# Fetching the down weights of experts 4 and 5 without waiting for the first gather, in a two-layer transformer kernel

## The chip, the cores and the metric

One core of a Trainium2 chip runs the kernel. The metric is the device time of one execution in microseconds (us). Runs of one kernel agree within about 0.3%.

## What is computed

The input x is (1, 512, 1024) float32: 512 tokens. Two layers follow each other. Each is a mixer (attention of two kinds side by side) and then a mixture of experts, both with a plain residual:

```python
for layer in range(2):
    h = h + mixer(rmsnorm(h, attn_norm[layer]))      # even_mixer, then odd_mixer
    h = h + hierarchical_moe(rmsnorm(h, ffn_norm[layer]), ...)
return rmsnorm(h, final_norm)
```

The experts are 32 per layer, in 4 groups of 8. Each token goes to the best group and there to its best 2 experts, with weights:

```python
g_idx = argmax(t @ w_group + b_group)
top_v, top_i = top_k(router logits of that group, 2)
gates = p_group * softmax(top_v)          # zero for all other experts
a, u = t @ w_gate[e], t @ w_up[e]         # 1024 -> 256
y = y + (silu(a) * u * gates[e]) @ w_down[e]   # 256 -> 1024
```

Each expert's three matrices are 1 MB each, so that a layer's experts are 96 MB of weights that are read once.

## The kernel before, in words

It is written by hand in five instruction streams, one per engine, which meet at semaphores: SyncE (sp) issues the large transfers, GpSimd (pool) the gathers, scatters and small loads, TensorE (pe) multiplies, VectorE (dve) and ScalarE (act) do the rest. Instructions of an engine go out in program order, so a wait holds up all that stands behind it in its own stream.

**Attention and routing.** After a layer's attention, `mixer_out` on TensorE multiplies by the output weights (line 825), and between these products transposes the new rows (line 846), makes the router logits (line 860) and counts the ranks of the tokens in their experts (lines 872, 873, 880). Matmuls whose result nobody reads (`stay_busy`, line 889) fill the waits. VectorE turns the logits into indices (its last step is line 1479). The normed, transposed rows that the router multiplies lie in the buffer hnT.

**Experts.** Expert e has 64 places for rows. For each expert in turn:

- GpSimd gathers its rows from DRAM (line 587) into one of four buffers Xg. The first four gathers are issued together once the indices are there; each further one when its buffer is free.
- TensorE transposes them (line 940); VectorE copies them out with the gain (line 1564); TensorE multiplies by the gate and up weights (lines 951, 952), ScalarE and VectorE make the hidden rows, TensorE transposes these (line 958) and multiplies by the down weights (lines 964, 966); VectorE copies the result (line 1579) and GpSimd scatters it to DRAM (line 592).
- TensorE starts an expert when its gate and up weights have landed. Rows of expert e+1 are transposed while expert e is under way.

**Weights and their slots.** There are six slots for experts' weights (`SLOT_W`, `SLOT_D`). Each is a 2 MB buffer for gate and up and a 1 MB one for down. The down slots of experts 4 and 5 are the two halves of hnT, which is why they can only be loaded once the router logits of the layer are done (semaphore s_lg). `load_gate_up` (line 413) issues two transfers of 1 MB, `load_down` (line 418) one. Expert e, from 6 on, is loaded into the slot of an earlier expert: its gate and up weights when TensorE has done that expert's gate and up products (s_gu), its down weights when the down products are done (s_y).

**The place of the change.** `before_routing` holds SyncE's stream between attention and experts. It ends with the gate and up weights of expert 5, a wait for the first gather of the layer (semaphore s_g[0], counted up by 16 when a transfer has landed), a wait for the layer's four chunks of router logits, and the down weights of experts 4 and 5. Behind it stands `experts`, whose first entry waits for TensorE to be done with expert 0's gate and up weights. The function runs once per layer, so the wait stands twice in the program.

Of the kernel before, what the change touches and what calls it, by code (L numbers as in the profile page):

```python
# [93 lines left out]
def trunk(nc, x, attn_norm, ffn_norm, final_norm, e_w_in, e_b_f, e_w_out, o_w_in, o_q_norm, o_kv_norm,  # L94
# [71 lines left out]
    with ctx:  # L166
# [3 lines left out]
        def sem(name):  # L170
            return ctx.enter_context(nc.semaphore(name))
# [181 lines left out]
        s_g = [sem(f"rows_gathered{i}") for i in range(4)]  # L353
# [35 lines left out]
        def _(sp):  # L389
# [5 lines left out]
            def load_cols(buf, dst, src, c0, width):  # L395
                sp.dma_start(dst, src[:, :, c0:c0 + width]).then_inc(s_ld[buf], 48)
# [13 lines left out]
            def load_gate_up(lay, e):  # L410
                gate_up, _, done, _ = expert_slot(lay, e)
                for v, at, count in ((wg_v[lay], 0, 16), (wu_v[lay], 2048, 32)):
                    sp.dma_start(gate_up[:, at:at + 2048].rearrange("p (h x) -> p h x", h=2), v[e])\  # L413
                      .then_inc(done[0], count)

            def load_down(lay, e):
                _, down, _, done = expert_slot(lay, e)
                sp.dma_start(down, wd_v[lay][e]).then_inc(done[0], 16)  # L418

            def before_routing(lay, w_out):  # L420

                sp.wait_ge(s_qk, 64 * (lay + 1))
                load_cols("Q", flatQ.rearrange("p (k n) -> p k n", k=KD), w_out, 0, 512)
                load_cols("K", flatK.rearrange("p (k n) -> p k n", k=KD), w_out, 512, 512)
                sp.wait_ge(s_pv, 8 * (lay + 1))
                load_down(lay, 3)
                sp.wait_ge(s_og, 8 * lay + 4)
                load_gate_up(lay, 4)
                rows = h_dram[lay].rearrange("(s h) d -> s (h d)", h=2)
                for c in range(C):  # L430
                    sp.wait_ge(s_oga, 8 * lay + 5 + c)
                    sp.dma_start(rows[128 * c:128 * c + 128, :], h[:, c, :]).then_inc(s_hst, 16)
                sp.wait_ge(s_og, 8 * lay + 8)
                load_gate_up(lay, 5)
                sp.wait_ge(s_g[0], 16 * (8 * lay + 1))
                sp.wait_ge(s_lg, C * (lay + 1))
                load_down(lay, 4)
                load_down(lay, 5)
# [64 lines left out]
            sp.wait_ge(s_pj, 24)  # L503
            load_gate_up(0, 3)
            before_routing(0, ewout_v)
            experts(0)
            sp.wait_ge(s_gu, 24)
# [22 lines left out]
            sp.wait_ge(s_pj, 52)  # L530
            load_gate_up(1, 3)
            before_routing(1, owout_v)
            experts(1)
            further_tiles(1)
# [1205 lines left out]
```

## Time and profile before

| | |
|---|---|
| median of 3 runs | 1150.05 us (1149.61 to 1153.0) |
| the profiled execution | 1149.53 us |
| its span, first to last instruction | 1147.7 us |
| PE busy | 1029.5 us, 90% |
| VectorE, ScalarE, GpSimd busy | 402.8, 255.2, 161.0 us |
| moved by DMA | 268.65 MB, mean 234 GB/s |
| granted TensorE clock, mean | 0.965 of full |

The span runs through attention of layer 0, its experts (from about 346 us to 582 us), attention of layer 1, its experts (from about 882 us to 1118 us) and the final norm. PE's share is an average: a TensorE that is busy 90% of the time may still be waiting at the places that set the end. For the stages the profile gives windows (busy time of each engine, the granted clock, the DMA engines' share and GB/s within a stretch), and the chain of waits that ended last, which tells at each moment what the end hung on.

### The profile page before, as it was taken

The page shows a single profiled execution, that of the slowest core. Times are in us where ns is not written, and L with a number is a line of the kernel's source. Part 1 is how long each engine was busy: PE and PEld are TensorE (multiplying, and loading weights), DVE is VectorE, ACT ScalarE, POOL GpSimd, SP SyncE. Part 2 cuts the span into 40 slices and gives each one's busy share as a digit, 9 for nine tenths or more (in the row PEclk, how much of TensorE's full clock was granted, in tenths as well). Part 3 has the DMA queues.
Part 4 walks back from the last instruction along what each step waited for, and adds up shares of the span by engine and source line. Part 5 has one row for each costly group of instructions (what it writes and reads, how often), then busy time and mean ns, then how long its engine had stood idle before and what let it go on. Part 6 is the DMA issues. An engine that isn't in the chain of part 4 may idle for free.

```text
span 1147.7 us, 13123 instructions
## 1 busy us (share of the span) xinstructions
PE 1029.5 (90%) x5160; PEld 549.3 (48%) x5160; DVE 402.8 (35%) x1115; ACT 255.2 (22%) x667; POOL 161.0 (14%) x170
## 2 busy tenths in 40 slices
PE   5999999999999999988838998989999999998890
PEld 3344644464455555444414647446455555554440
DVE  3122810362264322222234326458035432322225
ACT  3121710262121111000012226447012111110012
POOL 2000000001003333222111000000102233222210
PEclk9999999999999999999978999999999999998995
DMA  9610202215238999999978210023325999999975
GB/s 330 228 60 25 75 1 110 74 74 190 92 128 339 411 408 410 410 410 411 413 298 289 74 73 1 9 100 116 122 110 194 382 410 410 411 411 410 411 303 230
DMA packets 78814, 268.65 MB, mean 234 GB/s; under 512 B 13664, under 2 KB 17872, under 8 KB 69786
## 3 DMA queue, kind: packets, MB, share of 16 engines
q1 hardware_dynamic: 67056, 248.17, 55.3%
q0 software_dynamic: 11696, 19.62, 4.9%
q8 instruction: 42, 0.69, 0.2%
q14 instruction: 20, 0.16, 0.0%
HBM read 261.41 MB, written 23.10 MB: 248 GB/s over the span
## 4 chain that ended last, share of the span: by engine, by line
PE 71%; DMA 17%; DVE 5%; SPq 4%; ACT 2%; issue 1%; DVEq 0%; POOLq 0%; ACTq 0%
PE bank L735 13%; PE bank L951 12%; DMA W<-in_moe_w_up 10%; PE bank L825 10%; PE bank L747 9%; PE bank L964 7%; PE bank L766 5%; PE bank L777 2%; PE bank L940 2%; PE bank L793 2%; SPq L418 2%; DMA Q<-in_moe_w_up 2%; DMA oT<-in_moe_w_up 2%; PE bank L1071 2%; SPq L413 1%; PE bank L958 1%
## 5 line engine op out<-in xcount | busy, mean ns | idle before, releaser
L951 PE MATMUL bank<-W,K 128*64 128x256 f32 x768 | 186.1, 398 | 27.5 <-DMA W<-in_moe_w_up 25.7
L952 PE MATMUL bank<-W,K 128*64 128x256 f32 x768 | 186.2, 398 | 0.0
L951 PEld LDWEIGHTS bank<-W,K 128*64 128x64 f32 x768 | 105.6, 142 | 87.8 <-DMA W<-in_moe_w_up 29.5
L735 PE MATMUL bank<-hnT,W 128*128 128x512 f32 x336 | 145.1, 593 | 0.8 <-ACT hnT L1145 0.8
L1559 DVE SCALAR_TENSOR_TENSOR PT<-bank,V,PT 64x256 f32<-64x256 f32 x64 | 31.4, 490 | 273.8 <-ACT PT L1209 273.8
L952 PEld LDWEIGHTS bank<-W,K 128*64 128x64 f32 x768 | 105.6, 142 | 0.0
L735 PEld LDWEIGHTS bank<-hnT,W 128*128 128x128 f32 x336 | 63.5, 190 | 80.5 <-issue 79.5
L964 PE MATMUL bank<-D,PT 128*64 128x512 f32 x192 | 92.6, 604 | 0.7 <-ACT PT L1213 0.7
L966 PE MATMUL bank<-D,PT 128*64 128x512 f32 x192 | 92.6, 604 | 0.0
L587 POOL DMA_INDIRECT K<-rows,V x64 | 66.4, 1037 | 147.7 <-DVE V L1479 124.1
L1209 ACT ACTIVATE PT<-bank,V 64x256 f32<-64x256 f32 x64 | 29.9, 468 | 254.4 <-PE bank L952 251.8
L766 PE MATMUL bank<-K,Q 128*128 128x256 f32 (+3 forms) x256 | 70.4, 417 | 6.1 <-ACT K L1158 3.4
L1173 ACT ACTIVATE P<-P,nm 128x256 f32<-128x256 f32 (+3 forms) x128 | 68.3, 535 | 14.6 <-DVE nm L1353 14.1
L747 PE MATMUL bank<-W,hnT 128*128 128x512 f32 (+2 forms) x256 | 71.4, 440 | 0.0
L825 PE MATMUL bank<-K,oT 128*128 128x512 f32 x128 | 59.2, 600 | 0.0
L825 PE MATMUL bank<-Q,oT 128*128 128x512 f32 x128 | 56.5, 594 | 1.4 <-ACT oT L1189 1.4
L592 POOL DMA_INDIRECT expert_rows<-V x32 | 32.6, 1018 | 163.9 <-DVE V L1579 163.9
L592 POOL DMA_INDIRECT expert_rows<-K,V x32 | 32.5, 1017 | 163.7 <-DVE K L1579 163.7
L747 PEld LDWEIGHTS bank<-W,hnT 128*128 128x128 f32 x256 | 40.4, 190 | 31.1 <-issue 31.1
L1213 ACT ACTIVATE PT<-bank 128x128 f32<-128x128 f32 x64 | 17.8, 278 | 156.0 <-PE bank L958 156.0
L1353 DVE CUSTOM_DVE_ANT_0 P<-bank,cst 128x128 f32<-128x128 f32 (+1 forms) x96 | 46.0, 489 | 15.0 <-PE bank L766 13.8
L766 PEld LDWEIGHTS bank<-K,Q 128*128 128x128 f32 x256 | 40.7, 190 | 21.6 <-DVE nm L1353 6.0
(226 smaller groups left out, 1431.2 us busy)
## 6 DMA issues: line engine op xcount, KB each, us to landing
D<-in_moe_w_down SPq DMA_DIRECT2D x48, 1024.0 KB, 22.1
W<-in_moe_w_gate SPq DMA_DIRECT2D x48, 1024.0 KB
W<-in_moe_w_up SPq DMA_DIRECT2D x48, 1024.0 KB
hnT<-in_moe_w_down SPq DMA_DIRECT2D x16, 1024.0 KB, 21.7
W<-in_e_w_in SPq DMA_DIRECT2D x5, 2048.0 KB
Q<-in_moe_w_gate SPq DMA_DIRECT2D x8, 1024.0 KB
Q<-in_moe_w_up SPq DMA_DIRECT2D x8, 1024.0 KB
oT<-in_moe_w_gate SPq DMA_DIRECT2D x8, 1024.0 KB
```

What stands on the lines that cost most here:

```text
L587: pool.indirect_dma_start(out=dst, out_offset=None, in_=h_dram[lay], in_offset=bass.IndirectOffsetOnAxis(ap=idx_col, axis=0), bounds_check ...
L592: pool.indirect_dma_start(out=y_dram[lay], out_offset=bass.IndirectOffsetOnAxis(ap=idx_col, axis=0), in_=src, in_offset=None, bounds_check ...
L735: last = nc.tensor.matmul(b[:, :], w[:, k, 128 * fb:128 * fb + 128], hnT[:, k, :], start=(k == 0), stop=(k == KD - 1))
L747: last = nc.tensor.matmul(b[:, at:at + width], hnT[:, k, 128 * c:128 * c + 128], w[:, k, c0:c0 + width], start=(k == 0), stop=(k == KD - 1))
L766: nc.tensor.matmul(bank[b % 3][:, 0:n], Q[:, u, 128 * i:128 * i + 128], K[:, kv, k0:k0 + n], start=True, stop=True).then_inc(s_qk, 1)
L825: last = nc.tensor.matmul(bank[g % 2][:, :], oT[:, k, 128 * c:128 * c + 128], w_out[half][:, k, :], start=(k == 0), stop=(k == KD - 1))
L951: nc.tensor.matmul(bank[2 + e2][0:64, 0:256], xt, w[:, at:at + 256], start=first, stop=end)
L952: last = nc.tensor.matmul(bank[2 + e2][64:128, 0:256], xt, w[:, 2048 + at:2304 + at], start=first, stop=end)
L964: nc.tensor.matmul(bank[5 + e2][0:64, :], hT[e2][:, 64 * c:64 * c + 64], d[:, 1024 * c:1024 * c + 512], start=(c == 0), stop=(c == 1))
L966: last = nc.tensor.matmul(bank[5 + e2][64:128, :], hT[e2][:, 64 * c:64 * c + 64], d[:, 1024 * c + 512:1024 * c + 1024], start=(c == 0), st ...
L1173: nc.scalar.activation(blk, blk, ACT.Exp, bias=nm[:, b % 8:b % 8 + 1], scale=-1.0, accum_out=den[:, b % 8:b % 8 + 1]).then_inc(s_exp, 1)
L1353: nc.vector.tensor_tensor_reduce(out=P[:, u % 2, p_col(f, i):p_col(f, i) + n], in0=bank[b % 3][:, 0:n], in1=cst[:, at + width - n:at + wid ...
```

## The change

The wait for the first gather is taken out; the wait for the router logits stays. Both layers use the function, so two waits go.

```diff
                 sp.wait_ge(s_og, 8 * lay + 8)
                 load_gate_up(lay, 5)
-                sp.wait_ge(s_g[0], 16 * (8 * lay + 1))
                 sp.wait_ge(s_lg, C * (lay + 1))
                 load_down(lay, 4)
                 load_down(lay, 5)
```

On no engine does an instruction move. On SyncE, at the end of `before_routing` in layer 0, where oT is the gate and up slot of expert 5, hnT the down slots of experts 4 and 5, and the last W row the gate weights of expert 6, the rows read (a minus is before, a plus the change):

```order
 L413 DMA oT<-in_moe_w_gate 128x2x1024 [waits mixer_projected]
 L413 DMA oT<-in_moe_w_up 128x2x1024
-L418 DMA hnT<-in_moe_w_down 128x2048 [waits router_logits,rows_gathered0]
+L418 DMA hnT<-in_moe_w_down 128x2048 [waits router_logits]
 L418 DMA hnT<-in_moe_w_down 128x2048
 L413 DMA W<-in_moe_w_gate 128x2x1024 [waits gate_up_done]
```

Of the two semaphores before the first down load only that of the router logits is left; layer 1 reads the same.

## Rows read from the trace of the kernel before

**Rows 1.** The page: GB/s moved in 40 equal slices of the span.

```profile
GB/s 330 228 60 25 75 1 110 74 74 190 92 128 339 411 408 410 410 410 411 413 298 289 74 73 1 9 100 116 122 110 194 382 410 410 411 411 410 411 303 230
```

**Rows 2.** Windows, the long stretches: busy us (instructions) per engine, clock, DMA share, GB/s.

```profile
361.00:578.00 217.00, 200.17 (x1358) 107.39 (x1356) 61.79 (x116) 21.89 (x59) 59.61 (x60) 0.98 1.02 409
...
897.00:1104.00 207.00, 193.65 (x1298) 103.53 (x1294) 59.82 (x112) 21.14 (x57) 56.68 (x56) 0.97 1.02 410
```

**Rows 3.** Windows of 1 us, same columns (PE, PEld, DVE, ACT, POOL first).

```profile
343.00:344.00 1.00, 1.00 (x3) 0.48 (x3) 0.62 (x5) 0.31 (x2) 0.39 (x1) 1.00 0.45 172
344.00:345.00 1.00, 1.00 (x3) 0.38 (x2) 0.83 (x7) 0.00 (x0) 0.71 (x1) 1.00 0.07 29
345.00:346.00 1.00, 1.00 (x4) 0.38 (x2) 0.97 (x5) 0.00 (x0) 0.98 (x1) 1.00 0.49 135
...
349.00:350.00 1.00, 1.00 (x13) 0.79 (x11) 0.44 (x1) 0.00 (x0) 1.00 (x1) 1.00 0.99 418
...
360.00:361.00 1.00, 1.00 (x6) 0.65 (x8) 0.48 (x1) 0.47 (x1) 0.00 (x0) 1.00 0.07 25
...
362.00:363.00 1.00, 1.00 (x8) 0.44 (x6) 0.44 (x1) 0.02 (x1) 0.00 (x0) 1.00 1.01 414
...
880.00:881.00 1.00, 1.00 (x3) 0.38 (x2) 0.83 (x7) 0.00 (x0) 0.74 (x1) 1.00 0.21 70
```

**Rows 4.** Timeline of SyncE's DMA queue: start us, us, line, transfer.

```profile
346.73 0.81 SPq L418 DMA_DIRECT2D hnT<-in_moe_w_down  x2
352.09 0.38 SPq L413 DMA_DIRECT2D W<-in_moe_w_gate  x1
...
360.01 0.37 SPq L413 DMA_DIRECT2D W<-in_moe_w_gate  x1
...
882.60 0.82 SPq L418 DMA_DIRECT2D hnT<-in_moe_w_down  x2
```

**Rows 5.** The chain that ended last: start us, us, what.

```profile
337.01 1.22 PE bank L860 x8
...
343.61 3.10 DMA K<-rows,V
346.76 0.76 PE bank L940 x4
...
879.63 2.95 DMA K<-rows,V
```

**Rows 6.** Waits of SyncE, whole span: us in total, times, longest.

```profile
SPq L418 <- DMA K<-rows,V: 16.7, 2, 8.4
```

**Rows 7.** The page's DMA issues: count, size of each, median us to landing.

```profile
hnT<-in_moe_w_down SPq DMA_DIRECT2D x16, 1024.0 KB, 21.7
```

**Rows 8.** Line 587, layer 0's fourth and fifth gather: issue and time to landing.

```profile
L587 POOL DMA_INDIRECT K<-rows,V x1: 998/998/998, 347.6 to 347.6; - x1
DMA to landing us min/median/max: 7.4/7.4/7.4
...
L587 POOL DMA_INDIRECT K<-rows,V x1: 1357/1357/1357, 349.0 to 349.0; - x1
DMA to landing us min/median/max: 6.4/6.4/6.4
```

**Rows 9.** Timeline of PE: start us, us, line, [idle before, releaser].

```profile
342.82 3.68 PE L889 MATMUL bank<-cst 128*128 128x512 f32 x8
...
1019.85 0.43 PE L951 MATMUL bank<-W,K 128*64 128x256 f32 x1 [2.02 <-DMA W<-in_moe_w_up]
...
1020.60 0.63 PE L951 MATMUL bank<-W,K 128*64 128x256 f32 x1
...
1023.96 0.38 PE L951 MATMUL bank<-W,K 128*64 128x256 f32 x1
...
1024.18 0.38 PE L951 MATMUL bank<-W,K 128*64 128x256 f32 x1
...
1079.25 0.43 PE L951 MATMUL bank<-W,K 128*64 128x256 f32 x1 [1.86 <-DMA W<-in_moe_w_up]
```

## The prediction

> **What bounds the kernel now.** I read the forty slices of the page first. In each layer the DMA engines move 408 to 413 GB/s through one long stretch, slices 14 to 20 and 33 to 38 [rows 1], and nowhere else as much. Those are the expert stages. The stage windows say the same of them: DMA share 1.02 at 409 and 410 GB/s over 217 and 207 us [rows 2], while PE is busy for 200 of the 217 us. Once such a stretch has begun, its end is fixed by its bytes. What counts is therefore when the stretch **begins**, and who decides that.
>
> The windows of 1 us at the head of the first layer's stage answer it [rows 3]. The transfers for expert 5 run out in window 343:344 (172 GB/s), 344:345 is nearly empty (29 GB/s), 349:350 is full again (418 GB/s) with the down weights of experts 4 and 5 and then the gate and up weights of expert 6. At 360:361 the engines are empty a second time (25 GB/s), and from 362:363 (414 GB/s) they stay full to the end. So the long stretch starts with the loads of expert 7. SyncE issues those at 360.01 [rows 4], when PE has finished the gate and up product of expert 1. All slots are full before that: a weight load can't come earlier than PE frees a slot.
>
> When does PE start? The chain of waits reads [rows 5]: the last router product at 337.01, routing on VectorE, the gather of expert 0's rows issued at 343.61, on the chain for 3.10 us as DMA, and PE's transposes of those rows at 346.76. In the second layer the same gather is issued at 879.63 and holds the chain for 2.95 us. From there everything up to expert 7's loads is PE's own chain. The first gather is on the path that sets the end, in both layers.
>
> **The change part by part.** It removes one wait of SyncE per layer. The waits of the DMA queue's own engine price it as seen from SyncE: 16.7 us, twice, at most 8.4 [rows 6]. No instruction is added or moved on any engine. SyncE's next wait there is for the router logits, whose last four of eight products stand in the 1.22 us from 337.01 [rows 5], so the two loads go out at about 338.3 in place of 346.73, and at about 874.4 in place of 882.60 [rows 4].
>
> *Gain on the weights: nothing.* Each load is 1024 KB [rows 7], the two together 2.10 MB, 5.1 us at 410 GB/s. Now they fill the hole behind expert 5's transfers, from about 343.5 to 348.7. But the next weight load (expert 6, 352.09) waits for PE's first product and the one after it (expert 7, 360.01) for the second [rows 4]. The engines were empty before expert 7's loads even with the down weights sent late (25 GB/s in 360:361), so sending these early only makes the second hole longer. The down weights themselves are late for nobody: they are used by experts 4 and 5, five experts after the one now starting, and no wait of PE for them shows at either place. Cover for this zero: PE's chain from gather 0 to the end of expert 1's product, some 13 us from 346.76 to 360. If the cover were gone, the 5.1 us would be a gain, see the rivals.
>
> *Cost on the gather.* Gather 0 is issued at 343.61 into engines that were about to fall empty. Afterwards it is issued just as the down weights begin to move, and they keep the engines full for 5 us. The trace of before has gathers issued beside such a load [rows 8]: the fourth of the same layer, issued at 347.6, took 7.4 us to land, the fifth, issued at 349.0, took 6.4. Against 3.10 us that is 3.3 to 4.3 us more. This is the upper bound, because those two had a load beside them for all of their way. For gather 0 the load ends at about 348.7, or 349.5 with the bytes of the gathers; then it finds empty engines again. Issued at 343.61 and landed soon after 349.5, it is 2.9 us later than 346.7. In the second layer expert 5's transfers run until about 880, past the issue of the gather (880:881 is the first slack window, 70 GB/s [rows 3]), so that the down weights with the gathers last to about 886: landing 3.5 us later than the present end, 879.63 + 2.95 = 882.6. The lower bound is zero, if the gather's few bytes pass between the weights; a gain below zero is excluded, as the same gather can't be faster with more beside it. I take 2.9 and 3.5, nearest to the rows of loaded gathers and cut by the length of the load: 6.4 us.
>
> Here the Trainium skill speaks against a cost (DMA: Bandwidth & Descriptors, section Queues, rings and completion order): each DMA engine takes turns between the queues that have work, a packet at a time. By that rule a short gather on a queue of its own would be held up by about its own size in others' packets, some tenths of a microsecond, and the sum would be close to zero. The rows of the 7.4 us and 6.4 us gathers don't agree with so small a delay, though they don't show where the time is spent. I go by the rows.
>
> *Cost on PE's clock.* PE fills its wait for the gather with products that nobody reads, 3.68 us from 342.82 [rows 9], so up to 346.5. Now it sits idle for about 3 us more behind them, then does 0.75 us of transposes and waits again for VectorE. What a gap can do shows in the second layer, in the same rows: after 2.02 us of waiting the product runs at full speed, then from 1020.60 to 1023.96 eight pairs of matmuls take 3.36 us, where the next pair starts 0.22 us after the one before (eight of them 1.76): 1.6 us lost at the lower granted clock, 1.2 GHz. A gap of 1.86 us at 1079.25 has no such slow products behind it, so a gap of that size may cost or not. The bounds are 0 and 1.6 us per layer. A 3 us gap is longer than both, but part of the slow time may lie inside the gap where it costs nothing; I take half, 0.8 us per layer, 1.6 us in all. It adds in full, as the first product is on PE's chain.
>
> *Sum.* 2.9 + 3.5 + 1.6 = 8.0 us. The profiled execution took 1149.53 us (span 1147.7 plus 1.8 around it); it stands 0.5 us under the median of the runs, 1150.05. From the execution 1157.5, from the median 1158. I forecast **1157.5 us**, 0.65% slower. Nothing later gives it back: the stretch after 362 has its full bytes to move at 410 GB/s whenever it starts, and it starts later by what PE starts later.
>
> **The rivals.**
> *The gather gets its turns (not slower).* Gather 0's packets pass between those of the weights and it lands within 1.5 us of now. For it: its bytes are few (135 GB/s in 345:346 [rows 3], when gathers alone moved, are 135 KB in that microsecond), and the load ends soon. Against it: the 6.4 and 7.4 us of rows 8. The price is 0 to 1.5 us per layer, no clock loss: 1150 to 1153, around 1151. It decides below 1.7 us per layer, where two layers stay within what can be told from no change. Chance 0.18.
> *The hole is filled and pays (faster).* If the engines were the only limit of the stage, moving 2.10 MB into an empty place would take up to 5.1 us from each layer: 1149.5 − 10.2 = 1139.3, or part of it. The point from which it decides: expert 7's loads would have to stand in the queue before it runs empty. They are issued at 360.01 and the windows show the queue at 25 GB/s there, so it speaks against itself by 1 to 2 us in each layer. Chance 0.05.
> *Both costs in full (slower still).* The gather takes the whole 7.4 us, because weights that were begun are finished first, and PE's first product runs wholly at the lower clock: 2 × (4.3 + 1.6) = 11.8, so 1161.3. For it: the rows of the gathers as they stand. Against it: the load beside gather 0 ends after 5 us. Chance 0.15.
> *The change does nothing* would need SyncE to be held at that place by something else. The other wait is over at 338.3, so I count this under the first rival.
>
> **How the numbers follow.** My own case, a gather 2.3 to 4.0 us late per layer with some or no clock loss, is 1154 to 1160.5 and has 0.62. A measurement of this kernel can tell about 0.3%, 3.5 us, from no change; that is the band of "same", 1146.6 to 1153.5. Slower: 0.62 + 0.15 = 0.77; same: 0.18; faster: 0.05. The range goes from 1151, in the middle of the first rival, to 1161.5, which takes in the full price of the third; outside are the faster case and the lower half of the first rival, some 0.15 together.
>
> **What would show it.** In the changed profile the two down loads are issued near 338.3 and 874.4, and the wait for the gather is gone from SyncE. The engines are full to about 349, then empty until expert 6's loads. The chain shows the first gather as DMA for 5.5 to 7 us in each layer, PE's first transposes near 349.7 and 886.1, expert 7's loads near 363.5 and 899, and the long stretch beginning 3 to 4 us later with unchanged length. A row of slow first products would show the clock term. I am wrong if gather 0 still lands in about 3 us, or if the long stretch begins no later, or ends sooner than it began later.

## The result and the profile after

The changed kernel took 1163.46 us in the median (1162.2 to 1164.68), the kernel before beside it 1150.64 us. The ratio is 1.0105, with a 95% interval of 1.0093 to 1.0118: about 12 us slower. The forecast was 1157.5 us with a range up to 1161.5. The direction was right, the loss was larger than the range allowed for. The profiled execution has a span of 1161.8 us, 14.1 more than before. That is more than the 12 us of the ratio because the profiled execution of before (1149.53 us) is among its fastest: 27 executions of that kernel beside the first experiments took 1149.4 to 1156.7 us, a wider spread than the 0.3% given at the start. Differences of marks below are therefore those of single executions, and the ratios say what a change costs on the average. In the rows of the changed kernel the line numbers behind the removed line are lower by one: its line 586 is 587 of before, 939 is 940, 950 is 951.

The timeline of SyncE's DMA queue in both layers, start and duration in us, answers to [rows 4]:

```profile
338.42 0.82 SPq L418 DMA_DIRECT2D hnT<-in_moe_w_down  x2
357.73 0.38 SPq L413 DMA_DIRECT2D W<-in_moe_w_gate  x1
367.33 0.37 SPq L413 DMA_DIRECT2D W<-in_moe_w_gate  x1
...
881.77 0.86 SPq L418 DMA_DIRECT2D hnT<-in_moe_w_down  x2
900.49 0.38 SPq L413 DMA_DIRECT2D W<-in_moe_w_gate  x1
910.09 0.37 SPq L413 DMA_DIRECT2D W<-in_moe_w_gate  x1
```

The down weights go out 8.3 us earlier, as the change says. The loads of expert 7 go out at 367.33 instead of 360.01, 7.3 us later. The chain of waits (start, us, what) answers to [rows 5]:

```profile
343.83 7.06 DMA K<-rows,V
350.94 0.76 PE bank L939 x4
351.73 0.70 DVE K L1563
352.57 0.66 PE bank L950
353.26 0.39 PE bank L950
...
362.65 0.41 PE bank L950
363.08 0.41 PE bank L950
...
887.10 6.59 DMA K<-rows,V
893.74 0.76 PE bank L939 x4
```

The gather of expert 0's rows now holds the chain for 7.06 us in the first layer and 6.59 in the second, where it held it for 3.10 and 2.95. The pieces at line 950 are the matmuls of TensorE's gate and up products, as far as each holds the chain: 0.39 to 0.41 us, where at full clock it is 0.20 to 0.21. That happens in the product of expert 0 (from 352.57) and again in that of expert 1 (from 362.65), in both layers. The windows of 1 us (busy time of PE, PEld, DVE, ACT, POOL, then the granted clock, DMA share, GB/s) show the load and the clock, against [rows 3]:

```profile
349.00:350.00 1.00, 0.00 (x0) 0.00 (x0) 0.00 (x0) 0.00 (x0) 0.00 (x0) 1.00 0.99 371
350.00:351.00 1.00, 0.06 (x1) 0.06 (x1) 0.00 (x0) 0.00 (x0) 0.00 (x0) 1.00 0.45 162
...
353.00:354.00 1.00, 1.00 (x8) 0.66 (x6) 0.62 (x2) 0.00 (x0) 0.00 (x0) 0.50 0.33 78
...
363.00:364.00 1.00, 1.00 (x8) 0.59 (x6) 0.00 (x0) 0.00 (x0) 0.00 (x0) 0.50 1.01 414
...
366.00:367.00 1.00, 1.00 (x12) 0.57 (x8) 0.00 (x0) 0.00 (x0) 0.00 (x0) 1.00 0.00 0
...
370.00:371.00 1.00, 1.00 (x10) 0.66 (x11) 1.00 (x7) 0.28 (x1) 0.14 (x1) 1.00 0.98 406
```

TensorE has nothing at all in 349:350, the clock column stands at 0.50 (1.2 GHz) in 353:354 and in 363:364, and the DMA engines are empty in 366:367, before expert 7's loads. The long stretch begins at about 369.5 instead of 361.9. It runs at the same rate as in [rows 2], so its length is unchanged:

```profile
369.00:586.00 217.00, 200.10 (x1359) 107.45 (x1356) 61.16 (x115) 21.87 (x59) 59.59 (x60) 0.98 1.02 409
```

So the span divides at four marks per kernel. Before: first gather issued 343.61, landed 3.10 later, expert 7's loads 13.30 after that (360.01); in the second layer 879.63, 2.95, 13.29 (895.87). After: 343.83, 7.06, 16.44 (367.33); 887.10, 6.59, 16.40 (910.09). What lies between is the same: from 360.01 to 879.63 is 519.62, from 367.33 to 887.10 is 519.77; from expert 7's loads of the second layer to the end 251.83 and 251.71. The 14.1 us are therefore 3.96 + 3.64 = 7.6 for the gathers, 3.14 + 3.11 = 6.25 between landing and expert 7's loads, where nothing but the slow products has changed, and 0.25 in all elsewhere. The 6.25 are of two parts: from expert 6's loads to expert 7's it is 9.60 us in both layers instead of 7.92, which is 1.68 each for the second product; the first product is left with 1.46 and 1.43.

### The profile page after: what moved, and what is told of

It reads as the page before. It is cut to its first block, busy times and chain, and to the rows that moved or that the text cites. A ratio compares the mean times of both kernels' runs of the same rounds, so it can differ in the third digit from the quotient of the medians.

```text
span 1161.8 us, 13121 instructions
## 1 busy us (share of the span) xinstructions
PE 1036.0 (89%) x5160; PEld 551.8 (47%) x5160; DVE 402.8 (35%) x1115; ACT 255.1 (22%) x667; POOL 160.4 (14%) x170
## 4 chain that ended last, share of the span: by engine, by line
PE 70%; DMA 18%; DVE 4%; SPq 4%; ACT 2%; issue 1%; DVEq 0%; ACTq 0%
PE bank L950 13%; PE bank L734 12%; DMA W<-in_moe_w_up 10%; PE bank L824 10%; PE bank L746 9%; PE bank L963 6%; PE bank L765 5%; PE bank L939 2%; PE bank L776 2%; SPq L418 2%; DMA Q<-in_moe_w_up 2%; PE bank L792 2%; DMA oT<-in_moe_w_up 2%; PE bank L1070 2%; SPq L413 1%; PE bank L957 1%
## 5 line engine op out<-in xcount | busy, mean ns | idle before, releaser
L950 PE MATMUL bank<-W,K 128*64 128x256 f32 x768 | 192.4, 408 | 27.6 <-DMA W<-in_moe_w_up 25.8
L951 PE MATMUL bank<-W,K 128*64 128x256 f32 x768 | 192.4, 408 | 0.0
L950 PEld LDWEIGHTS bank<-W,K 128*64 128x64 f32 x768 | 108.5, 146 | 91.5 <-DMA W<-in_moe_w_up 29.4
L951 PEld LDWEIGHTS bank<-W,K 128*64 128x64 f32 x768 | 108.5, 146 | 0.0
L1172 ACT ACTIVATE P<-P,nm 128x256 f32<-128x256 f32 (+3 forms) x128 | 68.3, 535 | 14.6 <-DVE nm L1352 14.1
L939 PE MATMUL bank<-cst,K 128*128 128x128 f32 x256 | 47.9, 309 | 8.0 <-DMA K<-rows,V 8.0
L1563 DVE TENSOR_TENSOR K<-bank,V 128x512 f32<-128x512 f32 x64 | 44.3, 692 | 21.8 <-PE bank L939 20.0
```

The lines of the kernel that those rows point to most:

```text
L939: last = nc.tensor.transpose(bank[e2][:, 128 * k:128 * k + 128], src.rearrange("p (x k) -> p k x", k=4)[:, k, :], ident)
L950: nc.tensor.matmul(bank[2 + e2][0:64, 0:256], xt, w[:, at:at + 256], start=first, stop=end)
L951: last = nc.tensor.matmul(bank[2 + e2][64:128, 0:256], xt, w[:, 2048 + at:2304 + at], start=first, stop=end)
L1172: nc.scalar.activation(blk, blk, ACT.Exp, bias=nm[:, b % 8:b % 8 + 1], scale=-1.0, accum_out=den[:, b % 8:b % 8 + 1]).then_inc(s_exp, 1)
```

## The experiments

The theory to test: the weights gain nothing by being early; the first gather is late because of the load beside it; the slow products come from the gap in which TensorE waits for it. The rivals: the gather alone costs, or the slow clock alone, or the begin of the long stretch isn't what sets the end. All ratios are to the kernel before on the same chip, whose median beside these runs was near 1152 us. A ratio of 1.001 is about 1.15 us.

### The gap bridged

```diff
                 last.then_inc(s_ws, 1)
-                stay_busy(4, 512)
+                stay_busy(8, 512)
```

This on top of the change.

> The change with four more of the products that nobody reads (3.7 us more, to about 350.4) on TensorE before it waits for the first gather, in both layers. If the slow first and second products in the changed kernel come from TensorE's idle gap before the gather, they run at full speed here: expert 7's loads go out near 364.3 instead of 367.33 and near 907 minus the first layer's gain, some 3.0 us less per layer, in all about 1157.5. If the gather's delay alone made the loss and the slow products cost nothing that counts, no change: 1163.5. The gather itself should stay at 6.6 to 7.1 us in both theories.

Measured: 1159.75 us, ratio 1.0068 (1.0045 to 1.009), some 4 us better than the change and 8 us worse than before. In the second layer it is as the clock theory has it: the chain shows the gather and then a first and second product at full speed, expert 7's loads (905.86) 13.25 us after TensorE's first transposes (892.61), as before.

```profile
885.55 7.01 DMA K<-rows,V
```

In the first layer the unread products themselves ran at the lower clock, so that they lasted longer than the gather (8.81 us instead of 7.11), and the second product was slow once more:

```profile
342.73 8.81 PE L888 MATMUL bank<-cst 128*128 128x512 f32 x16
351.38 0.63 PE L939 MATMUL bank<-cst,K 128*128 128x128 f32 x4
```

The 7.8 us that the ratio leaves are close to the gathers' 7.6, but this execution doesn't divide in that way. In the second layer 3.9 us are left, and there the gather is all of it (7.01 us instead of 2.95). The first layer's 6.1 us are 4.6 at TensorE's start, of which the overrun of the unread products is a part, and 1.5 in the second product. Bridging a gap doesn't give back what made it.

### The clock alone

```diff
                 last.then_inc(s_ws, 1)
-                stay_busy(4, 512)
```

This in the kernel before, the wait in place.

> The kernel before without the four products that nobody reads behind the routing (3.7 us from 342.82): TensorE is idle for 3.9 us until the gather lands at 346.7 as before; no transfer moves. This is the clock term alone. If a gap of 4 us costs what the changed kernel shows (7 slow pairs in the first product, 8 to 9 in the second), the first gather stays at 3.1 us and each layer loses about 3.0 us: 1156.5. By the 0.8 us per layer of the prediction 1152.2. If the gap is harmless by itself, 1150.6.

Measured: 1156.29 us, ratio 1.0038 (1.0023 to 1.0052), 4.4 us. The gather is untouched (first row, from the chain), TensorE's gap before the transposes is 3.82 us, and most of the first product is slow, its first matmul 0.66 us instead of 0.40, eleven of its sixteen pairs in the first layer and fourteen in the second; from the timeline of PE (line numbers again one lower):

```profile
345.05 3.14 DMA K<-rows,V
```

```profile
348.24 1.12 PE L939 MATMUL bank<-cst,K 128*128 128x128 f32 x4 [3.82 <-DMA K<-rows,V]
350.24 0.66 PE L950 MATMUL bank<-W,K 128*64 128x256 f32 x1 [0.88 <-DVE K L1563]
```

From these transposes to expert 7's loads it is 15.9 us, in the second layer 16.5, against 13.25: 2.7 and 3.3 us for the clock alone in this execution; their sum of 6.0 is at the upper end of the interval, whose middle is 2.2 per layer. The prediction's 0.8 per layer falls, and with it its bound of 1.6. The loss isn't placed as in the change: here it lies in the transposes (1.12 us instead of 0.75) and the first product, and the second ran at full speed in both layers.

### A later TensorE without load or gap

The same doubling of the unread products as in the first experiment, but in the kernel before.

> The kernel before with four more such products: TensorE is held until about 350.2 though the gather lands at 346.7, a later start of 3.4 us per layer at full clock, with no more load beside the gather. If the end follows TensorE's start one to one, 2 x 3.4 = 6.9 us more: 1157.5. If the long DMA stretch has slack at its head, less, down to 1150.6.

Measured: 1157.84 us, ratio 1.0056 (1.0039 to 1.0073), 6.5 us, as expected. A later start of TensorE alone moves the end. The marks say it closest: from expert 7's loads to the second layer's gather (365.25 to 884.92) it is 519.67 us, before 519.62, and from those of the second layer to the end 251.89, before 251.83. The profile has one more thing: expert 7's loads at 365.25 in the first layer, 9.60 after expert 6's (355.65), and 7.92 in the second. The second product was slow in the first layer though TensorE had had no gap before the transposes for its first, so that 1.7 us of this execution's loss aren't from the later start.

### Half the load

```diff
-                sp.wait_ge(s_g[0], 16 * (8 * lay + 1))
                 sp.wait_ge(s_lg, C * (lay + 1))
                 load_down(lay, 4)
+                sp.wait_ge(s_g[0], 16 * (8 * lay + 1))
                 load_down(lay, 5)
```

> Only the down weights of expert 4 are fetched early (1 MB), those of expert 5 still wait for the gather. The load beside the gather ends near 346.3 instead of 349. If the gather is held as long as the load lasts, it lands near 347.5 (3.7 to 4.5 us after its issue at 343.7), TensorE's gap stays under 1.5 us with no slow products, and the time is 1152 to 1154. If a gather beside any load takes its 6.5 to 7 us, it lands near 350.5 and the time is near that of the change, 1161 to 1163.

Measured: 1156.06 us, ratio 1.0041 (1.0023 to 1.0058). The gathers took, by the chain,

```profile
343.54 5.34 DMA K<-rows,V
...
881.62 4.53 DMA K<-rows,V
```

which is longer than the 3.7 to 4.5 us expected in the first layer, and far from 6.5 to 7. Half of the load gives about half of the delay: 2.2 and 1.6 us instead of 4.0 and 3.6. The loss is above the 1152 to 1154 expected, partly because the second product of the second layer was slow (expert 7's loads 9.60 us after expert 6's).

### Smaller pieces

This on top of the change.

```diff
-                load_down(lay, 4)
-                load_down(lay, 5)
+                for e in (4, 5):
+                    _, down, _, done = expert_slot(lay, e)
+                    for q in range(4):
+                        sp.dma_start(down[:, 512 * q:512 * q + 512], wd_v[lay][e][:, 512 * q:512 * q + 512])\
+                          .then_inc(done[0] if q == 3 else s_piece[e - 4], 16)
```

TensorE waits for the pieces' own semaphores before the down products of experts 4 and 5.

> The change with each of the two down loads issued as four transfers of a quarter of the columns, so that a row piece is 2 KB instead of 8 KB; same bytes, same place. If the gather is late because it takes turns with large pieces, it lands well before the load ends: issue to landing 4 to 5 us instead of 7.06 and 6.59, and the time falls by 4 to 6 us, to 1158 to 1160. If it is late because it stands behind bytes that are already under way in the engines, whatever their pieces, it still lands with the end of the load, 6.5 to 7 us, and the time stays at 1163 within 1 us.

Measured: 1161.79 us, ratio 1.0083 (1.0058 to 1.0108). The chain has the gathers at

```profile
343.96 6.41 DMA K<-rows,V
...
885.22 6.14 DMA K<-rows,V
```

half a microsecond less than with large pieces, not the 2 to 3 that turns with large pieces would explain. The size of the row pieces is at most a small part of the cause. How many pieces an engine takes from one queue before it turns to the next isn't seen here, so a turn counted in bytes rather than pieces isn't excluded.

### One layer only

```diff
-                sp.wait_ge(s_g[0], 16 * (8 * lay + 1))
+                if lay:
+                    sp.wait_ge(s_g[0], 16 * (8 * lay + 1))
```

> The wait is taken out in the first layer only. If each layer pays by itself (7.3 us at expert 7's loads of the first layer, the rest in the second), the time is 1150.6 + 7 = 1157.5 and the second layer's gather takes 2.9 to 3.0 us. If the second layer's loss hung on the first layer's, the whole 13 us or none of it would show.

Measured: 1157.16 us, ratio 1.0037 (1.0022 to 1.0052). The first layer pays by itself: gather 6.95 us, expert 7's loads at 365.76, 5.75 later than before, and the span of 1153.0 is 5.3 longer. In this execution the second product ran at full speed, which is why it is less than the 7.3 of the change. It is also the fastest of ten executions (1154.82 us, the median is 1157.16); by the ratio the cost is 4.3 us, 2.5 to 6.0 by the interval, which just reaches half of the change's 12.

### The loads with the gather instead of ahead of it

```diff
-                sp.wait_ge(s_g[0], 16 * (8 * lay + 1))
+                sp.wait_ge(s_idx, lay + 1)
```

> The two down loads wait for the indices (ready just before the first gather is issued, 343.6) instead of for the landed gather. The gather then starts beside empty engines, and the weights come 2 us behind it. If only load that is under way before the gather's packets delays it, the gather lands in 3.1 to 3.7 us and the time is that of before, 1150 to 1152. If any load that overlaps it holds it until the load is over, it lands in 6 to 7 us and the time is 1160 to 1163. Neither theory expects a gain over before, because the weights have nothing to gain by being early.

Measured: 1163.57 us, ratio 1.0095 (1.007 to 1.012). SyncE's queue and the chain:

```profile
343.41 0.81 SPq L418 DMA_DIRECT2D hnT<-in_moe_w_down  x2
```

```profile
343.67 7.66 DMA K<-rows,V
...
885.52 7.61 DMA K<-rows,V
```

The gather starts into engines that are running empty and takes longer than in the change. But the weights didn't come 2 us behind it as expected: released by the same indices, they were issued 0.26 us ahead of it in both layers. So it isn't enough that no load is under way when the gather is issued, if one comes with it. A load that comes clearly behind the gather was not tried with the first one, but the kernel before has the case in its second gather (line 587, issue and time to landing, first layer):

```profile
L587 POOL DMA_INDIRECT K<-rows,V x1: 1025/1025/1025, 345.0 to 345.0; - x1
DMA to landing us min/median/max: 2.8/2.8/2.8
```

In the second layer it was issued at 881.0 and took 2.7 us. The down weights were issued at 346.73 and 882.60, some 1.7 and 1.6 us behind these gathers and before they had landed, and didn't delay them. The wait on the landed gather is safe; that nothing may be issued until then is not so.

### A longer load

Expert 5's gate and up weights moved behind the same wait for the indices, ahead of the two down loads:

```diff
+                sp.wait_ge(s_idx, lay + 1)
                 load_gate_up(lay, 5)
-                sp.wait_ge(s_g[0], 16 * (8 * lay + 1))
                 sp.wait_ge(s_lg, C * (lay + 1))
```

> Expert 5's gate and up weights and the down weights of experts 4 and 5 are all issued with the indices, so that 4.2 MB run beside the first gather instead of 2.1. If a gather beside a load lands when the load is over, it takes 11 to 12 us and expert 7's loads go out near 372. If a gather beside full engines takes some 7 us whatever is still to come, as the gathers in the long stretch do (6.2 to 7.4), it takes 6.5 to 7.7 us and expert 7's loads go out between 364.5 and 367.5.

Measured: 1163.48 us, ratio 1.0102 (1.007 to 1.0135), from two executions. The chain, and a window while the load was still moving at 381 GB/s, 5 us after the gather had landed:

```profile
343.89 6.69 DMA K<-rows,V
...
886.14 6.32 DMA K<-rows,V
```

```profile
356.00:357.00 1.00, 1.00 (x8) 0.64 (x6) 0.00 (x0) 0.00 (x0) 0.00 (x0) 0.50 0.94 381
```

Beside full engines this gather takes 6 to 8 us even when the load goes on for longer. It doesn't wait for the load's end. That the change's gather landed just as its load ran out was then a coincidence of sizes: with twice the load it landed no later.

### The weights later still

```diff
-                sp.wait_ge(s_g[0], 16 * (8 * lay + 1))
+                sp.wait_ge(s_gu, NE * lay + 1)
```

> The kernel before with the two down loads held back further, until TensorE is done with expert 0's gate and up product (352.09), so that they stand just ahead of expert 6's gate and up weights. The gather keeps its 3.1 us. If the down weights' moment is free only while the engines still run empty before expert 7's loads (issued 360.01), this is too late: 4.2 MB from about 354 last to 364.5, where the long stretch now begins at 361.9, 2.6 us later per layer, 1156. If their moment never counted, 1150.6.

Measured: 1157.59 us, ratio 1.0047 (1.0025 to 1.0069), 5.4 us. The engines are no longer empty when expert 7's loads are issued (361.05), and from there nothing is gained by having these loads in the queue:

```profile
361.00:362.00 1.00, 1.00 (x8) 0.70 (x8) 0.44 (x1) 0.47 (x1) 0.00 (x0) 1.00 1.00 414
362.00:363.00 1.00, 1.00 (x8) 0.29 (x4) 0.74 (x2) 0.00 (x0) 0.00 (x0) 1.00 1.04 426
```

From expert 7's loads of the second layer (901.36) to the end (1155.6) it is 254.2 us here, 2.4 more than the 251.8 of before, and from those of the first layer to the second layer's gather (882.18) 1.5 more: bytes that still had to be moved. The rest of this execution's 7.9 us has nothing to do with the weights: the four unread products ran slow in both layers (5.38 us instead of 3.68) and held TensorE's start by 1.2 and 1.4 us, and the second product of the second layer was slow. That the time came out near the 1156 expected is therefore in part luck. So the moment of the two down loads is free within limits. Issued at 346.73 they cost nothing that shows, 6.4 us later they cost some 4 us in the two layers together, 8 us earlier the gather pays.

### A version that beats both

The theory says that expert 7's loads set the end. In the kernel before they wait for a product that TensorE begins late: it first waits 1.39 us for ScalarE and VectorE, to transpose expert 0's hidden rows. Expert 1's product doesn't need them.

```diff
                     gate_up(e % 2, w).then_inc(s_gu, 1)
+                    if e == 1:
+                        pe.wait_ge(s_hid, base + 1)
+                        hidden_transposes(0).then_inc(s_ht, 1)
...
-                    pe.wait_ge(s_hid, base + e + 1)
-                    hidden_transposes(e % 2).then_inc(s_ht, 1)
+                    if e:
+                        pe.wait_ge(s_hid, base + e + 1)
+                        hidden_transposes(e % 2).then_inc(s_ht, 1)
```

> The kernel before with the wait in place; on TensorE expert 1's gate and up product goes ahead of the transposes of expert 0's hidden rows, so that it doesn't sit out the 1.39 us for ScalarE and VectorE. Expert 7's loads go out about 1.9 us earlier in each layer (358.1 instead of 360.01). If the beginning of the long DMA stretch is set by these loads, as the theory has it, the two layers give up to 3.5 us back: 1147 to 1148.5. If the stretch is set by anything else, or the queue's own 2 us of delay hides it, 1150.6.

Measured: 1150.11 us against 1151.95, ratio 0.9974 (0.9959 to 0.9989), 1.8 us faster by the medians and 3 by the ratio. Expert 7's loads go out 6.03 us after expert 6's instead of 7.92. In the profiled execution the four unread products ran slow and outlasted the gather (5.38 us instead of 3.68, on the timeline of PE):

```profile
343.14 5.38 PE L889 MATMUL bank<-cst 128*128 128x512 f32 x8
```

so a last kernel has three of them, `stay_busy(3, 512)`, and is otherwise the same.

> Expert 1's product ahead of expert 0's hidden transposes, the wait in place, and three instead of four unread products behind the routing. With four, the profiled run had TensorE busy with them until 348.4 at the lower clock while the gather had landed at 346.9. If that overrun costs on average, the time falls by up to 1 us under that of four, to 1148 to 1149.5. If the shorter bridge brings slow first products instead, 1150 to 1153.

Measured: 1149.53 us against 1151.65, ratio 0.9981 (0.9969 to 0.9994). Both intervals lie below 1, by a few tenths of a per cent; the two can't be told apart, so what the overrun costs stays open. Its profiled span (1147.6) equals that of before: expert 7's loads went out at 358.44, 1.6 us earlier, the expert stage's results were fetched at 588.53 instead of 589.76, and by the second layer's first gather (880.31 instead of 879.63) it had been lost again in the attention between. I didn't follow that loss; between 700 and 760 us the granted clock was 0.97 of full instead of 1.00, which is of that size.

## Why the prediction was wrong, and where it was right

- **What bounds the kernel: right.** The chain from the first gather over TensorE's first two products to expert 7's loads sets where the long stretch begins, and the stretch keeps its length. The distances between the marks on either side of it agree to 0.15 us, and a TensorE held up without load or gap moved the end as well.
- **Gain on the weights: right.** Moving them 8.3 us forward gained nothing; the engines were empty before expert 7's loads as foretold (0 GB/s in 366:367).
- **Cost on the gather: right in kind, 1.2 us too small.** Foretold 2.9 + 3.5 = 6.4, measured 3.96 + 3.64 = 7.6. The step that failed is the cut by the length of the load. It put the end of the load a microsecond too early (162 GB/s were still moving in 350:351), and the load's end isn't what the gather waits for: with 4.2 MB beside it, it landed over 6 us before the load was over, with 1 MB some 2 us after. The upper bound, taken from the gathers of [rows 8], held: 3.3 to 4.3.
- **Cost on PE's clock: the term that broke the range.** Foretold 0.8 us per layer, at most 1.6, measured 3.1 in the profiled execution. Two steps failed. The price of one slow stretch, taken from a gap of 2.0 us behind which eight pairs were slow, was halved because part of the stretch might lie inside the gap; behind the gaps of 4.2 and 3.8 us the first product was slow from its first matmul on and lost 1.46 and 1.43 us, nearly the full 1.6. And the second product, 10 us later, stood in the sum at nothing, without a reason; it was slow as well, for 1.68 us in each layer. With both terms as measured the sum is 7.6 + 6.25 = 13.9 of the execution's 14.1. The experiment on the clock alone shows that the gap by itself costs more than the bound: 2.2 us per layer by its ratio, 2.7 and 3.3 in its profile, though there in the transposes and the first product.
- **The rule of turns.** The Trainium skill (DMA: Bandwidth & Descriptors, section Queues, rings and completion order) would have had the gather pass between the weights' packets; the first rival was built on that mechanism. In the executions quoted here ten first gathers with 2 MB or more beside them took 6.1 to 7.7 us, five without (two of them before, two without unread products, one in the last kernel) 2.9 to 3.3. The rule isn't refuted: in the longest load the gather did land while weights were still moving. But the delay of 3.2 to 4.7 us isn't the tenths of a microsecond worked out from it, and it isn't in proportion to the piece size that could be changed (6.1 to 6.4 us with pieces a quarter as large).
- **The rivals.** The third, both costs in full, was the nearest: it had 11.8 us, of which 4.3 + 1.6 per layer, measured 3.8 + 3.1. It had been given 0.15. Its sum is near in part by luck: its reason, that weights once begun are finished first, doesn't fit the longest load, and its clock term was the first product's alone.

What stays open is why some second products are slow, and with it 3.4 us of the 14.1. In most executions profiled here expert 7's loads come either 7.9 us after expert 6's or 9.5 to 9.6 (7.1 or 8.7 with the weights later still): slow in both layers of the change, in one layer of six experiments, in none of the kernel before, of that without unread products, of the one-layer kernel, of that with the loads at the indices and of the last two (6.0). It occurs without any gap before the first product. The change moves these products to where they were slow; that it must is not shown. Nor is it shown where in the engines the gather waits.

## What to carry to other kernels

A transfer that is on the critical path and small should have the DMA engines to itself, not only when it is issued: a load issued with it cost as much as one issued 5 us before, while one issued 1.7 us behind a second gather cost that gather nothing. Waiting until it has landed is the safe form. A bulk load held back for it costs nothing as long as the engines still run empty before the next load that someone waits for. Price a new gap on TensorE with both of its costs, the wait and the lower clock behind it, and look at every product up to the one that frees a slot. Extra bytes in an idle hole are worth nothing when the hole ends with a release, and the way to shorten such a hole is the release, as the last experiments did.

## What the hardware showed that was not expected

The same gather of some tens of rows took 2.9 to 3.3 us beside empty DMA engines and 6.1 to 7.7 us beside a load of 2 MB or more at some 400 GB/s, whether the load was under way already, issued at the same moment, cut into small pieces or twice as long. With 1 MB beside it, it took 4.5 and 5.3 us. Unread products meant to keep the clock up can themselves run at 1.2 GHz and then hold up the work behind them: the four at the end of the routing took 5.38 us instead of 3.68 in at least four of the profiled executions, and in two of these the gather that they bridged had landed before they were done.
